# RWKV stage of a hybrid decoder step: the first receptance tile among the back-projections, other banks, and a low-rank product that signals twice

## What is computed

```python
xr, xw, xk, xv, xa, xg = (h + xx * mu[j] for j in range(6))
r = xr @ w_rkv[0]                       # receptance
k = xk @ w_rkv[1]
v = xv @ w_rkv[2]
w_log = -softplus(-(w0 + tanh(xw @ w1) @ w2)) - 0.5      # decay
a = sigmoid(a0 + (xa @ a1) @ a2)                          # rate
g = sigmoid(xg @ g1) @ g2                                 # gate
kk = heads(k * k_k)
kk = kk * rsqrt(maximum(sum(kk * kk, -1), 1e-24))
k = k * (1.0 + (a - 1.0) * k_a)
y, s = rwkv7_scan(r, decay, k, v, -kk, kk * a, s0)        # 16 heads of 64
```

## Time and profile before

| | |
|---|---|
| time, median of 3 runs | 1598.32 us (1597.86 to 1598.56) |
| time of the profiled execution | 1598.63 us |
| its span, first to last instruction | 1596.9 us |
| TensorE busy | 1562.8 us, 98% of the span |
| VectorE, ScalarE busy | 1049.7 us (66%), 886.5 us (56%) |
| mean granted TensorE clock | 0.998 of full |
| RWKV stage up to its value projection | about 735 to 824 us of the span |

### The profile page before, as it was taken

The page is one execution under the profiler, slowest core; times in us unless marked ns, Lnnn a source line. Parts: engine busy times, 40 slices in busy tenths (PEclk is TensorE's granted clock), DMA queues, the critical chain, the costliest instruction groups (busy, mean ns, idle before and its releaser), DMA issues.

```text
span 1596.9 us, 37857 instructions
## 1 busy us (share of the span) xinstructions
PE 1562.8 (98%) x16256; PEld 1481.1 (93%) x16256; DVE 1049.7 (66%) x1722; ACT 886.5 (56%) x1700; POOL 257.1 (16%) x328
## 2 busy tenths in 40 slices
PE   9999999999999999999999999999999999999997
PEld 7998799999997999999788878999999997999997
DVE  7965677745757877557583647776569837767643
ACT  6846656633645666434552547665348647666433
POOL 7106350000110200003003320200010026400000
PEclk9999999999999999999999999999999999999999
DMA  9940466555754665553624102666558612665550
GB/s 251 287 136 29 134 181 177 184 194 185 240 157 132 200 185 185 188 182 93 189 96 132 30 7 85 172 185 201 185 167 264 185 55 65 177 180 185 188 168 28
DMA packets 245529, 250.10 MB, mean 157 GB/s; under 512 B 16270, under 2 KB 239284, under 8 KB 245300
## 3 DMA queue, kind: packets, MB, share of 16 engines
q1 hardware_dynamic: 237204, 224.78, 45.9%
q0 software_dynamic: 8016, 22.86, 4.9%
q10 hardware_dynamic: 144, 0.05, 0.0%
HBM read 229.75 MB, written 18.32 MB: 155 GB/s over the span
## 4 chain that ended last, share of the span: by engine, by line
PE 91%; ACT 4%; DVE 3%; issue 1%; DMA 0%; SPq 0%; DVEq 0%; ACTq 0%
PE ps L842 87%; PE ps L846 3%; ACT st L2065 1%; ACT vk L2065 1%; DVE acts L2777 1%; ACT tri L2065 1%; ACT acts L2065 1%; DVE tri L2769 0%; ACT hn L2065 0%; DVE acts L2769 0%; DVE st L2777 0%; DMA acts<-in_x_sample_dram 0%; PE ps L1808 0%; ACT w_gdn L2065 0%; DVE hn L2777 0%
## 5 line engine op out<-in xcount | busy, mean ns | idle before, releaser
L2769 DVE TENSOR_TENSOR w_mlp<-ring,w_mlp 128x1024 fp32r<-128x1024 f32 x256 | 311.6, 1224 | 119.7 <-ACT w_mlp L2065 113.4
L2065 ACT ACTIVATE w_mlp<-ring 128x1024 fp32r<-128x1024 f32 x256 | 269.3, 1053 | 207.1 <-PE ps L842 207.1
L842 PE MATMUL ps<-hn_split,w_mlp 128*128 128x264 f32 x3072 | 373.3, 284 | 0.0
L842 PE MATMUL ps<-h_split,w_mlp 128*128 128x264 f32 x3072 | 372.6, 284 | 0.0
L842 PEld LDWEIGHTS ps<-hn_split,w_mlp 128*128 128x128 f32 x3072 | 372.0, 188 | 0.3
L842 PEld LDWEIGHTS ps<-h_split,w_mlp 128*128 128x128 f32 x3072 | 371.6, 188 | 0.0
L2065 ACT ACTIVATE tri<-ps 128x264 f32<-128x264 f32 (+4 forms) x226 | 103.3, 466 | 183.1 <-PE ps L842 156.3
L842 PE MATMUL ps<-gdn_hi,w_gdn 128*128 128x264 f32 x896 | 165.7, 285 | 0.0
L842 PEld LDWEIGHTS ps<-gdn_hi,w_gdn 128*128 128x128 f32 x896 | 139.3, 188 | 0.8 <-issue 0.8
L842 PE MATMUL ps<-mixer_lo,w_gdn 128*128 128x264 f32 x448 | 126.9, 283 | 0.0
L2769 DVE TENSOR_TENSOR tri<-tri 128x264 f32<-128x264 f32 (+4 forms) x145 | 59.7, 413 | 101.4 <-ACT h_split L2065 100.6
(11 more groups left out here) (452 smaller groups left out, 2649.4 us busy)
## 6 DMA issues: line engine op xcount, KB each, us to landing
ring<-in_ffn_w_dram SPq DMA_DIRECT2D x128, 1024.0 KB, 5.4
ring<-in_gdn_w_in_dram SPq DMA_DIRECT2D x32, 1024.0 KB, 7.9
ring<-in_ml_w_in_dram SPq DMA_DIRECT2D x12, 1024.0 KB, 5.5
ring<-in_rw_w_rkv_dram SPq DMA_DIRECT2D x12, 1024.0 KB, 5.0
st<-in_state_gdn_S_dram POOLq DMA_DIRECT2D x2, 4096.0 KB, 23.5
ring<-in_gdn_w_out_dram SPq DMA_DIRECT2D x8, 1024.0 KB, 5.1
out_gdn_S_s_dram<-st SPq DMA_DIRECT2D x16, 512.0 KB, 7.0
st<-in_state_mlstm_C_dram POOLq DMA_DIRECT2D x1, 4096.0 KB, 20.3
```

Of the source, the lines that this page charges most:

```text
L842: return nc.tensor.matmul(out, lhsT, rhs, start=start, stop=stop)
L2065: return nc.scalar.activation(out, in_, f, bias=bias, scale=scale)
L2769: return nc.vector.tensor_tensor(out, in0, in1, op)
```

## The change

- The low-rank product of decay and rate signals `lo_mm` after its step k = 3 and again after k = 7, by 1 each time, where it signalled by 2 at the end. VectorE waits for the first before it writes the first four tiles of xg, and for the second before the other four.
- The eight pairs of back-projections use six banks in turn: 2 and 3, 4 and 5, 6 and 7 (`pair_bank`), where they used all eight from 0 on.
- Seven of the eight products of receptance tile 0 are moved among the pairs: k = 0 to 3 behind the third pair, k = 4 to 6 behind the sixth. `linear` is told that seven are `begun` and does the last.
- The hooks of the receptance projection stand later by one tile each, up to the second `sum_key_squares`: `decays_to_rows` after tile 1, `cumulate_decays` after tile 2, `sum_key_squares` after tiles 3 and 4. `states_to_keys` stay after tiles 5 and 7. ACT's work moves with them: `key_norms` stands behind tiles 4 and 5, where it stood behind 3 and 4, and the first copies of the states behind tile 6 instead of 5.
- The banks of these hooks are dealt anew.

```diff
-        LWT_BANKS, CUM_BANKS = (0, 1, 2, 3), (0, 1, 2, 3)
-        KK_BANKS, RST_BANKS = (4, 5, 6, 7, 6, 7, 0, 1), (0, 1, 2, 3, 2, 3, 4, 5)
+        LWT_BANKS, CUM_BANKS = (4, 5, 6, 7), (0, 1, 6, 7)
+        KK_BANKS, RST_BANKS = (0, 1, 6, 7, 2, 3, 6, 7), (0, 1, 2, 3, 2, 3, 4, 5)
...
+        def pair_bank(t, i):
+            return 2 + 2 * (t % 3) + i
...
-                last.then_inc(lo_mm, count.up(lo_mm, 2))
+                    if k % 4 == 3:
+                        last.then_inc(lo_mm, count.up(lo_mm))
...
+                receptance = count.units
+                pe.wait_ge(w_in[receptance % RING], 16 * wloads[receptance])
+
+                def first_receptance(k):
+                    b = (count.tiles + 2 * (KT - t) - 2) % 8
+                    if k == 0:
+                        pe.wait_ge(*last_read[b])
+                    pe.wait_ge(xj_ok, count.seen(xj_ok))
+                    mm(ps[b][:, 0:T], ring[:, receptance % RING, k, 0:P], xj[0][:, k, :], k == 0, False)
+
                 for t in range(KT):
-                    two = [(count.tiles + i) % 8 for i in range(2)]
+                    two = [pair_bank(t, i) for i in range(2)]
...
+                    if t == 2:
+                        for k in range(4):
+                            first_receptance(k)
+                    elif t == 5:
+                        for k in range(4, KT - 1):
+                            first_receptance(k)
...
-                       hooks={0.5: decays_to_rows, 0: cumulate_decays, 1.5: lambda: sum_key_squares(0), 1: lambda: sum_key_squares(4),
+                       begun=KT - 1,
+                       hooks={0: decays_to_rows, 1.5: cumulate_decays, 1: lambda: sum_key_squares(0), 2.5: lambda: sum_key_squares(4),
                               2: lambda: states_to_keys(0), 3: lambda: states_to_keys(4)})
...
-                    if n == 1:
+                    if n == 2:
                         for q in range(4):
                             ac.wait_ge(rcum_mm, count.seen(rcum_mm))
...
-                    elif n in (0, 2):
-                        if not n:
+                    elif n in (1, 3):
+                        if n == 1:
                             decay_rows()
-                        key_squares(2 * n)
-                        if n:
+                        key_squares(2 * n - 2)
+                        if n == 3:
                             weight_hi()
                             weight_hi()
-                    elif n in (3, 4):
-                        key_norms(4 * n - 12)
-                    elif n == 5:
+                    elif n in (4, 5):
+                        key_norms(4 * n - 16)
+                    elif n == 6:
                         states_to_keys(0)
                         weight_hi()
...
                     if n == 2:
-                        dv.wait_ge(lo_mm, 2)
+                        dv.wait_ge(lo_mm, 1)
...
+                        if n == 2 and k == 4:
+                            dv.wait_ge(lo_mm, 2)
```

More of the change, by code:

```diff
@@ L869, in norm, with linear @@
                     keep_busy(5, *[256] * 6, 128)
-            def linear(src, n_cols, evac, ready, hooks=()):
+            def linear(src, n_cols, evac, ready, hooks=(), begun=None):
                 for u in range(n_cols // UNIT):
@@ L877, in linear @@
                         b = count.tiles % 8
-                        pe.wait_ge(*last_read[b])
-                        for k in range(KT):
-                            if ready and u == 0 and t == 0:
+                        first = u == 0 and t == 0
+                        if not (begun and first):
+                            pe.wait_ge(*last_read[b])
+                        for k in range(begun if begun and first else 0, KT):
+                            if ready and first:
                                 pe.wait_ge(ready, count.seen(ready))
@@ L2557, in rwkv @@
                 for i, (r, f) in enumerate(((low, ACT.Tanh), (high, ACT.Copy), (slice(0, 80), ACT.Sigmoid), (slice(0, 80), ACT.Sigmoid))):
-                    ac.wait_ge(lo_mm, count.seen(lo_mm))
+                    if i != 1:
+                        ac.wait_ge(lo_mm, count.seen(lo_mm, 1 if i else 2))
                     act(lo[i][r, :], ps[3 + i][r, 0:T], f).then_inc(lo_ev, count.up(lo_ev))
@@ L2564, in rwkv @@
                 for n in range(KT):
-                    tile(4, n, ACT.Sigmoid, V_W0)
-                    tile(5, n, ACT.Sigmoid, V_A0)
+                    for i, dst, at in ((0, 4, V_W0), (1, 5, V_A0)):
+                        count.tiles += 1
+                        ac.wait_ge(lin_rdy, count.tiles)
+                        act(A(dst)[:, n, :], ps[pair_bank(n, i)][:, 0:T], ACT.Sigmoid, bias=vec2[:, at + n:at + n + 1]).then_inc(
+                            rk_ev, count.up(rk_ev))
                 exp_ln_table()
```

## The result

The changed kernel takes 1602.18 us (median of 20 runs, 1598.23 to 1606.13) where the kernel before takes 1598.63 (20 runs, 1597.66 to 1604.09). The ratio is 1.002, with a 95% interval of 1.0014 to 1.0026. The forecast was 1598.6 with a range of 1597.0 to 1600.6; the measured time lies 1.6 us above that range. It is the time of rival C, to which the prediction gave 0.07.

The account below looks back on a forecast made before the run. TensorE, 98% busy, was taken as the bound, with an ACT and VectorE chain from the key norms setting the later part; +0.2 up to the norms became +0.3 in total, 1598.6 us by the median, range 1597.0 to 1600.6.

Parts of the forecast that it names:

- rival C: 2.8 us idle before the third state bank drops TensorE's clock to 1.2 GHz: 3.6 us slower, 1602.2; chance 0.07.
- The sum up to the key norms: All terms from the gate products to ACT's first key norms: waits removed, later hook added, +0.2 (+0.25 by laying out products).
- first signal: Gate products: VectorE starts xg after half the low-rank product, so TensorE's wait at 767.15 goes, -0.8 us.
- The waits at 776, 785 and 795: TensorE waits at the first pair, decays_to_rows and tile 2, removed by other banks and later hooks: -0.95, -0.7, -0.7 us.
- the banks: Six banks for the pairs: the first pair no longer waits for the shift rows' read-out, -0.95 us.
- the pairs' pace: Eight pairs, held to ACT's read-out pace: receptance products fill the places where TensorE waited, -0.9 us.
- Changes between 64-row and full products: Seven receptance products among the pairs bring four more changes of row mode on TensorE, +0.7 us.
- The chain: 26.4 us of ACT and VectorE work from key norms to sample vectors sets the end; TensorE's waits there are slack.
- the tie at the third weight part: ACT has the third high weight part at 821.25, VectorE wants it at 821.24; can slip by 0.2 us.
- B: Freed waits stay free because VectorE has room between 805 and 830: -4.85 us, 1593.5; chance 0.06.
- D: First signal does nothing; gate products are held by something else and still start at 767.1: 1599.4; chance 0.07.
- Rival A: The forecast itself: the chain from the key norms sets the end, -0.5 to +0.9 us, 1597.8 to 1599.3; chance 0.80.

Follow-up runs that it names:

- e4: Kernel before with only the change's first part, lo_mm signalled in halves so VectorE starts xg after the first: 1597.47 us, ratio 0.9994.
- e1: Changed kernel with unread products filling both long TensorE waits, before the third state bank and before the sample vectors: 1598.20 us, ratio 0.9999.
- e2: Changed kernel with ACT's first key norms moved ahead of the read-out of receptance tile 4: 1598.15 us, ratio 0.9995.
- e9: Changed kernel with first key norms before tile 4's read-out and VectorE's decayed(0) behind the samples' small vectors: 1594.97 us, ratio 0.9976.
- e10: Changed kernel with only VectorE's decayed(0) moved later, behind the samples' small vectors; key norms stay behind tile 4: 1596.06 us, ratio 0.9988.
- e6: Changed kernel with four unread products filling only the second long wait, before the sample vectors: 1599.49 us, ratio 1.0009.
- e3: Kernel before with receptance tile 5 made of four products instead of eight, so TensorE waits longer at the states: 1598.83 us, ratio 1.0004.
- e5: Changed kernel with five unread products filling only the first long wait, before the third state bank: 1600.09 us, ratio 1.0010.
- e7: e2 plus four unread products in the wait before the sample vectors: 1596.24 us, ratio 0.9991.

## Why the prediction was wrong, point by point

**The sum up to the key norms was right.** +0.2 to +0.25 forecast, +0.25 measured, in every variant of the change with late norms (N - L is 41.91 in five traces). The terms: first signal -0.8 against -0.73 in e4. The waits at 776, 785 and 795 gone; what the terms of the banks and of the pairs' pace are worth one by one inside the change was not measured. Changes between 64-row and full products: in the changed kernel's trace each starts 0.09 us late and its first record lasts 0.1 longer, 0.2 a change in either direction, 0.8 for the four more; 0.7 was taken. The Trainium skill, "TensorEngine Tiling (Array Packing)", section "Key Properties", has it that a change of the tiling mode drains TensorE. A wait for the whole product ahead at each would have made it 0.4 more by the prediction's estimate; no row shows that.

**The chain was right.** Waits of 2.8 and 1.9 us forecast, 2.71 and 1.98 measured. V was to be 0.2 to 0.4 late; with the clock kept it is 0.25 (e1), and the tie at the third weight part did not slip. e2, e9 and e10 moved V by what they took from the chain.

**The step that failed is the chance of rival C**, 0.07 for the clock's fall at the wait of 2.8 us, and with it a sum that takes both long waits to cost TensorE no clock. With both filled the price is gone (e1, +0.25 us); bare, they cost 1.66 and 1.51. The argument was that the longest idle time in the trace is 1.41 us and that nothing shows what twice that does. This is no evidence for the clock staying up. It says that the trace is silent, and the forecast itself would leave the region in which the trace speaks, at two places. Nor was the trace silent. The 1.41 us of the earlier trace rows is the longest idle time with a product behind it; TensorE's last product ends at 1587.43, 9.5 us ahead of the end of the span. Here is the kernel before behind that product (columns as above):

```profile
1587.40:1592.00 4.60, 0.02 (x1) 0.00 (x0) 2.21 (x7) 3.55 (x12) 0.00 (x0) 0.99 0.29 118
1592.00:1596.90 4.90, 0.00 (x0) 0.00 (x0) 0.27 (x1) 0.00 (x0) 0.00 (x0) 0.50 0.31 110
```

The clock fell there, 4.5 us after the last product, and the slice of the earlier trace rows still shows a 9. The other traces have the same fall 1.9 us (e10) to 4.8 us (e1) after their last product. Of the two places only the first was considered; the 1.9 us at the sample vectors, also over 1.41, was not. Rival C's price, 3.6 us for one place, was too high for that place (1.66) and by accident right for both together (3.17). The mechanism that it named, tile 6 to the third weight part to VectorE, is what the trace shows: 1.69 us of VectorE's wait. That the median comes out at its 1602.2 is luck. The Trainium skill, "TensorE: Matmul & The Clock Gate", section "Part 1: The HAM clock gate", had the rule that an idle TensorE goes back to half the clock; the traces agree, at 0.50 in the stretches above.

**Rivals B and D** did not occur. (Rival A's upper end, 1598.32 + 0.9, is 1599.2 and not 1599.3, which changes nothing.) No trace with the chain whole kept the freed waits, and the gate products start right behind the low-rank ones.

## What to carry to other kernels

Removing waits ahead of a chain on other engines gathers them into one long wait behind, and a long wait on TensorE is not the same as several short ones: it can cost the clock, and then real time. Before such a change, add up where the waits will stand, and if one comes out longer than any that the trace has, price the lower clock as a likely case, or shorten the chain first (here by moving two pieces of other engines' programs, which together with the change gave 0.24%), or fill the wait with products that nobody reads (which gave back all but 0.25 us). And look at the clock by windows, over the end of the trace as well.

## What was not expected of the hardware

- At waits of 2.0 to 2.7 us the clock falls in some executions and not in others of the same program: 2.7 us were outlived in the profiles of e6 and e10, and not in that of the changed kernel, nor 2.6 us in that of e3. TensorE's end shows the same scatter, with 1.9 to 4.8 us from the last product to the fall. The changed kernel's runs spread from 1598.2 to 1606.1 in part for that reason; two falls explain up to about 3.2 us of it, and the kernel before has runs up to 1604.1 as well.
- The fall comes late. In the five cases in the stage TensorE had started again 0.1 to 1.5 us before (e3 at 815.6 behind a start at 815.46, e5 at 832.6 behind one at 831.08). So the clock has to be read behind the wait, and it is the products there that pay.
- It falls elsewhere, too, without such a wait. In the profile of e7 it was low at 174.9 and 1349.1, in the same part of the two DeltaNet layers, behind a stretch with no idle time over 0.5 us:

```profile
168.00:175.00 7.00, 6.97 (x126) 5.15 (x126) 6.16 (x10) 2.26 (x5) 0.00 (x0) 1.00 0.30 83
174.90:178.30 3.40, 3.40 (x32) 3.07 (x30) 0.00 (x0) 2.60 (x4) 0.00 (x0) 0.51 1.01 281
```

  The kernel before has a clock of 1.00 in the same two stretches. The one at 174.9 made the RWKV stage start 1.65 us later than in e2. What sets it off there stays open; no run was made for it.
- The page's row of the clock rounds to 9 in all slices, though the three stretches above, 13.6 us, and the end were at half. The mean clock with three places (0.993 against 0.998) is what shows it.
